# Layer normalisation of a convolution branch: the channel tiles summed before the product with the mean matrix

## The chip, the core and the metric

The kernel runs on one core of a Trainium2 chip. The metric is the device time of one execution in microseconds (us). The engines are PE (matrix products), DVE (VectorE), ACT (ScalarE), POOL (GpSimd) and SP, which only issues DMAs. Each has its own instruction queue that runs in order; they wait for each other through semaphores.

## What is computed

The reference is one step of a two-layer decoder for a prompt of 1024 tokens and 8 samples of 4 tokens, 1056 token columns in all. Layer 0 projects the input (1024 channels) onto 3352 columns that feed a convolution branch and a sparse attention branch. The part around the change is the convolution branch:

```python
y = lax.conv_general_dilated(u_ext, conv_w[:, None, :], (1,), 'VALID', ...) + conv_b   # 512 channels
return jax.nn.silu(layer_norm(y, ln_g, ln_b)) * jax.nn.silu(a_gate)

def layer_norm(x, g, b):
    mu = x.mean(-1, keepdims=True)
    var = jnp.square(x - mu).mean(-1, keepdims=True)
    return (x - mu) * lax.rsqrt(var + LN_EPS) * g + b
```

Mean and variance go over the 512 channels of a token. After it come attention, the output projection, the pooling layer 1 and its output projection.

## The kernel before

Activations lie with channels on the 128 partitions and tokens along the free axis. So the 512 channels of the convolution are four tiles `Y[:, i, :]` (i = 0 to 3) of 128 x 1056 float32, and the 1056 columns are worked on in three parts c = 0, 1, 2 of CH = 352.

The input projection runs over weight blocks m = 0 to 26 (function `one(m)` on PE, L754): 24 steps of three matmuls each (8 contraction tiles kk, three high and low products), into PSUM banks 0 to 2 for even m and 3 to 5 for odd m. The weight block m is rounded by ACT (`high`, L358, tile WH), its remainder taken by DVE or by POOL (`low`, L287, tile WL; POOL does m = 25 and 26 here), and after the products ACT moves the result out (`evac(m)`, L377).

The convolution's 30 later taps per tile are DVE instructions (L606) that run beside the projection and end shortly after block 23. The normalisation is then woven into blocks 24 and 25:

- `mean(c)` (L734): four float32 products of the matrix `meanm` (all entries 1/512) with `Y[:, 0..3, part c]`, added up in a PSUM bank. Each float32 product is issued as two matmuls, so a `mean` is 8 matmul instructions. The result is the mean over all 512 channels on every partition.
- DVE subtracts it from the four tiles (L641) and signals `s_yc`.
- `square(n)` on ACT (L417), n = 4c + i, writes the square of part c of tile i into one of the five buffers of SQ.
- `variance(c)` (L742): four products of `meanm` with the four squares, again 8 matmul instructions.
- `deviation(c)` on ACT (L424): the square root into RSTD. DVE takes the reciprocal (L646) and multiplies the four tiles (L648, `s_yn`).
- ACT applies scale, bias and SiLU to each whole tile (L484, `s_ys`), POOL multiplies by the gate (L346, `s_ya`).

The order on each queue is the order in the code. On PE: block 23, nine small transposes of the gates (L815), `mean(0)`, a wait for the gates' copy (`s_gtok`, L820, set by ACT at L470), block 24 with `mean(1)` before step kk = 2 and `mean(2)` before kk = 5, `variance(0)`, block 25 with `variance(1)` before kk = 3 and `variance(2)` before kk = 6, block 26, transposes of the value rows (L838), and then the attention. On ACT, block 24's evacuation and `high(26)` stand between the first five squares and the rest.

What follows blocks 24 to 26 is ordered by a planner for the attention, which the change does not touch; its first steps wait for the transposes of L838 and L832 (`s_tmt`) and for the convolution's last product (`s_ya`).

## Time and profile before

| | us |
|---|---|
| median of 3 runs | 1115.72 (1115.23 to 1117.55) |
| the profiled execution, its own time | 1120.08 |
| its span, first to last instruction | 1118.3 |
| PE busy | 1069.5 (96%) |
| DVE busy | 734.0 (66%) |
| ACT busy | 381.8 (34%) |
| POOL busy | 358.1 (32%) |

Busy time is a mean over stages with different limits. The stretch that matters here runs from 340 to 400 us of the span. All times at which something starts are counted from the span's start. The mean granted TensorE clock of the execution was 0.988 of full speed.

### The profile page before, as it was taken

What the parts mean: (1) busy time and instruction counts of PE and PEld (TensorE: products, weight loads), DVE (VectorE), ACT (ScalarE), POOL (GpSimd) and SP (SyncE); (2) the same over time, 40 slices, a digit from 0 to 9 for tenths busy, and PEclk for the clock granted to TensorE, in tenths of its full rate; (3) what the DMA queues carried; (4) which work ended last, traced back from release to release, by engine and by line L of the source; (5) the groups of instructions that cost most, each with busy time, mean ns of one, the idle gap of its engine ahead of it and who ended that gap; (6) DMA issues with size and microseconds to landing.
All of it is one profiled execution on the core that took longest, in us unless ns stands there. A gap on an engine that the chain in (4) does not pass through costs nothing.

```text
span 1118.3 us, 18968 instructions
## 1 busy us (share of the span) xinstructions
PE 1069.5 (96%) x7640; PEld 903.7 (81%) x7640; DVE 734.0 (66%) x1366; ACT 381.8 (34%) x805; POOL 358.1 (32%) x378
## 2 busy tenths in 40 slices
PE   6999999999999988999899989999999999999997
PEld 6888999999988954565556556787899999998875
DVE  3677889999885476676465766667546730258755
ACT  4201112123222554788466765411121121244000
POOL 3553630000000485665675454400023221309000
PEclk9999999999999988999899999999999999999998
DMA  8754511161421035300672027632221111142321
GB/s 235 239 162 144 167 60 38 40 227 51 122 43 20 1 101 174 115 2 1 229 258 81 2 94 236 162 130 85 76 76 39 55 38 32 32 151 76 128 84 61
DMA packets 85888, 113.73 MB, mean 102 GB/s; under 512 B 21952, under 2 KB 67144, under 8 KB 85727
## 3 DMA queue, kind: packets, MB, share of 16 engines
q1 hardware_dynamic: 71849, 69.51, 20.1%
q0 software_dynamic: 11776, 41.95, 11.1%
q10 hardware_dynamic: 2182, 1.16, 0.4%
q8 instruction: 55, 0.90, 0.3%
q14 instruction: 26, 0.21, 0.1%
HBM read 100.91 MB, written 16.64 MB: 105 GB/s over the span
## 4 chain that ended last, share of the span: by engine, by line
PE 85%; DVE 6%; issue 3%; DMA 3%; ACT 1%; POOL 1%; SPq 0%; DVEq 0%; POOLq 0%
PE PS L699 26%; PE PS L2059 15%; PE PS L1827 14%; PE PS L1314 5%; PE PS L1193 5%; PE PS L1175 4%; PE PS L687 3%; PE PS L1851 2%; PE PS L1231 2%; DMA TM<-in_state_win_kv 1%; DVE ACC L559 1%; PE PS L1840 1%; DMA XIN<-in_x_prompt 1%; PE PS L2039 1%; PE PS L1290 1%
## 5 line engine op out<-in xcount | busy, mean ns | idle before, releaser
L606 DVE SCALAR_TENSOR_TENSOR Y<-U,SM,Y 128x1024 f32<-128x1024 f32 x120 | 147.9, 1293 | 0.3
L699 PE MATMUL PS<-XH,WH 128*128 128x352 f32 (+1 forms) x648 | 146.9, 331 | 0.0
L699 PE MATMUL PS<-XL,WH 128*128 128x352 f32 (+1 forms) x648 | 144.0, 326 | 0.0
L699 PE MATMUL PS<-XH,WL 128*128 128x352 f32 (+1 forms) x648 | 143.2, 325 | 0.0
L699 PEld LDWEIGHTS PS<-XH,WH 128*128 128x128 f32 (+1 forms) x648 | 107.9, 186 | 2.7
L699 PEld LDWEIGHTS PS<-XH,WL 128*128 128x128 f32 (+1 forms) x648 | 108.1, 185 | 1.4
L699 PEld LDWEIGHTS PS<-XL,WH 128*128 128x128 f32 (+1 forms) x648 | 107.9, 185 | 1.4
L2166 POOL TENSOR_TENSOR WL<-WRAW,WH 128x1024 fp32r<-128x1024 f32 x14 | 37.4, 2675 | 210.8 <-ACT WH L2111 210.8
L559 DVE SCALAR_TENSOR_TENSOR ACC<-PS,SM,ACC 128x508 f32<-128x508 f32 x124 | 86.9, 741 | 25.1 <-PE PS L687 20.6
L290 POOL TENSOR_TENSOR WL<-WRAW,WH 128x1024 fp32r<-128x1024 f32 x12 | 28.7, 2391 | 231.8 <-ACT WH L363 231.1
L1314 PE MATMUL PS<-KV,Q 64*128 64x512 f32 (+3 forms) x384 | 79.4, 497 | 0.4 <-DVE STAT L1412 0.3
L2059 PE MATMUL PS<-XH,WH 128*128 128x352 f32 x360 | 77.2, 323 | 0.0
L2059 PE MATMUL PS<-XH,WL 128*128 128x352 f32 x360 | 77.1, 323 | 0.0
L2059 PE MATMUL PS<-XL,WH 128*128 128x352 f32 x360 | 77.1, 323 | 0.0
L1193 PE MATMUL PS<-PT,TM 128*64 128x256 f32 x528 | 72.5, 396 | 1.2 <-DVE BG L1508 1.1
L1827 PE MATMUL PS<-WOH,XH 128*128 128x512 f32 x224 | 71.0, 398 | 0.0
L1827 PE MATMUL PS<-WOL,XH 128*128 128x512 f32 x224 | 69.8, 393 | 0.0
L1827 PE MATMUL PS<-WOH,XL 128*128 128x512 f32 x224 | 69.5, 391 | 0.0
L1347 DVE COPY PT<-PS 128x512 f32<-128x512 f32 (+1 forms) x80 | 51.6, 645 | 21.6 <-PE PS L1175 9.1
L1569 POOL TENSOR_SCALAR PRS<-PRS,STAT,GTOK 128x512 f32<-128x512 f32 (+7 forms) x64 | 51.8, 820 | 41.5 <-DVE STAT L1408 41.1
L1314 PEld LDWEIGHTS PS<-KV,Q 64*128 64x128 f32 x384 | 39.4, 192 | 31.8 <-issue 18.0
L2059 PEld LDWEIGHTS PS<-XH,WL 128*128 128x128 f32 x360 | 61.0, 188 | 0.0
(333 smaller groups left out, 2040.3 us busy)
## 6 DMA issues: line engine op xcount, KB each, us to landing
WRAW<-in_w_in_even SPq DMA_DIRECT2D x16, 512.0 KB
WRAW<-in_w_in_odd SPq DMA_DIRECT2D x16, 512.0 KB, 4.1
TM<-in_state_win_kv SPq DMA_DIRECT2D x12, 512.0 KB
XIN<-in_x_prompt SPq DMA_DIRECT2D x8, 512.0 KB, 12.7
WRAW<-in_w_in_even SPq DMA_DIRECT2D x16, 256.0 KB
XR<-in_x_prompt SPq DMA_DIRECT2D x8, 512.0 KB, 3.5
layer_out<-R SPq DMA_DIRECT2D x8, 512.0 KB, 2.6
XR<-layer_out SPq DMA_DIRECT2D x8, 512.0 KB, 3.3
```

Source lines behind the costliest of these rows:

```text
L559: ins = v.scalar_tensor_tensor(acc, rows, weight, acc, ALU.mult, ALU.add)
L606: v.scalar_tensor_tensor(dst, src, CWT[:, i, t:t + 1], dst, ALU.mult, ALU.add).then_inc(s_cv, 1)
L687: ins = pe.transpose(PS[:, 6 + x, b * P:b * P + P], XC[:, load % 2, b, 256 * j + P * x:256 * j + P * x + P], ident[:, :])
L699: ins = pe.matmul(PS[0:mcols, 3 * slot + c, 0:CH], w[:, slot, kk, 0:mcols], x[:, kk, c * CH:(c + 1) * CH], start=(kk == 0 and n == 0), sto ...
L1175: ins = pe.transpose(PS[0:rows, 4 + a, c:c + 64], x[half, :], ident[half, half])
L1193: ins = pe.matmul(PS[hb:hb + HD, 6, 256 * gp:256 * gp + 256], v, PT[k % 2][0:rows, j, 256 * h:256 * h + 256], start=first, stop=(br == CMPB))
L1314: ins = pe.matmul(PS[:, row_bank[j] + b // 512, 0:w], Q[hb:hb + HD, g, tok(qt)], keys[:, k0 + b:k0 + b + w], start=True, stop=True)
L1347: ins = copy(out[:, :, :, a, :], PS[0:rows, 4 + a, 0:256 * k].rearrange("p (t x q) -> p t x q", t=k, q=64))
L1569: po.tensor_scalar(x, x, RCP[:, stat(p, h):stat(p, h) + 1], GTOK[:, qt, c:c + 1], ALU.mult, ALU.mult)\
L1827: ins = pe.matmul(PS[0:n, b0 + hf, :], x[:, kk, tok(tile)], w[:, kk, hf * 512:hf * 512 + 512], start=(kk == 0 and i == 0), stop=(kk == KT ...
L2059: ins = pe.matmul(PS[:, b0 + c, 0:CH], w[:, slot, kk, :], x[:, kk, c * CH:(c + 1) * CH], start=(kk == 0 and n == 0), stop=(kk == KT - 1 an ...
L2166: po.tensor_tensor(WL[:, m % 2, :, :], WRAW[:, m % 2, :, :], WH[:, m % 2, :, :].bitcast(F32), ALU.subtract).then_inc(s_wl2, 1)
```

## The change

The four tiles of Y are added up before the product with `meanm`, so that `mean(c)` is one product (two matmul instructions) instead of four. The sum goes into the tile SUM, which lies where SIG lay: POOL adds tiles 0 and 1, once the first two taps' tiles are done (`s_conv` 2), the sample columns are there (`s_cs`), and the stores of KWROW and SROW, which lie in the same place, have landed (`s_vrow`). DVE adds tiles 2 and 3 after its last tap. The squares are treated alike: DVE adds the four squares of a part with three instructions (`sum_squares`), and `variance(c)` is one product. All three means stand before step kk = 2 of block 24, `variance(0)` before kk = 6, and `variance(1)` and `variance(2)` before kk = 1 and 2 of block 25. `mean(2)` uses bank 5, so block 25 waits until DVE has read it (`s_yc` 3). ACT does all twelve squares and the first deviation before `high(26)`, and evacuates block 24 only after the three deviations. POOL's masks wait for the third mean. Three semaphores are reused from the input loads: s_half, s_sum and s_sqs are the semaphores s_xin6, s_xin7 and s_xin8 in the rows below; s_vrow is s_xin0.

```diff
--- before.py
+++ after.py
@@ -147,7 +147,7 @@
             "s_const", "s_rows", "s_pt", "s_stc", "s_idx", "s_small", "s_smalle", "s_xt", "s_xh", "s_xl")
         s_xin = sems(*[f"s_xin{i}" for i in range(NTT)])
         X_IN = 16
-        s_vrow, s_urow, s_rowst, s_winst, s_wc0, s_wc1 = s_xin[0:6]
+        s_vrow, s_urow, s_rowst, s_winst, s_wc0, s_wc1, s_half, s_sum, s_sqs = s_xin
         s_raw = sems("s_raw0", "s_raw1")
         s_xc = sems("s_xc0", "s_xc1")
         (s_cpt, s_cp, s_past, s_kcts, s_vcn) = sems("s_cpt", "s_cp", "s_past", "s_kcts", "s_vcn")
@@ -177,9 +177,15 @@
         VCN = at("VCN", [P, DB, P], F32, 105600)
         SMP = at("SMP", [P, 2, DS, DB], F32, GTOK_AT)
         NSQ = 5
+
+        def squared(n):
+
+            return 3 * (n // 4) + (1, 3, 2)[n % 4]
+
         SQ = at("SQ", [P, NSQ, CH], F32, 136256)
         RSTD = at("RSTD", [P, 3, CH], F32, 136256 + NSQ * CH * 4)
-        LN_BANK = ((6, 7, 6), (7, 6, 7))
+        LN_BANK = ((6, 7, 5), (6, 7, 6))
+        SUM = SIG
         TM = at("TM", [P, NTT, 768], F32, 164832)
 
         def values_copied(eng):
@@ -337,9 +343,14 @@
                 low(po, m)
                 if m < 8:
                     gather(m)
+            po.wait_ge(s_vrow, X_IN + 48)
+            po.wait_ge(s_conv, 2)
+            po.wait_ge(s_cs, 1)
+            po.tensor_tensor(SUM[:, :], Y[:, 0, :], Y[:, 1, :], ALU.add).then_inc(s_half, 1)
             for m in range(LOW_DVE[1], NM + 1):
                 po.wait_ge(s_wl, m)
                 low(po, m)
+            po.wait_ge(s_mean, 3)
             pool_masks(po, link)
             for i in range(4):
                 po.wait_ge(s_ys, i + 1)
@@ -417,12 +428,14 @@
             def square(n):
                 c, i = n // 4, n % 4
                 act.wait_ge(s_yc, c + 1)
-                if n >= NSQ:
-                    act.wait_ge(s_sqr, n - NSQ + 1)
+                if n == 8:
+                    act.wait_ge(s_sqr, 1)
+                elif n >= NSQ:
+                    act.wait_ge(s_sqs, X_IN + squared(n - NSQ))
                 act.activation(SQ[:, n % NSQ, :], Y[:, i, c * CH:c * CH + CH], ACT.Square).then_inc(s_sq, 1)
 
             def deviation(c):
-                act.wait_ge(s_sqr, 4 * c + 4)
+                act.wait_ge(s_sqr, c + 1)
                 act.activation(RSTD[:, c, :], PS[:, LN_BANK[1][c], 0:CH], ACT.Sqrt, bias=EPSC[:, :]).then_inc(s_stdc, 1)
 
             def rows_out(m):
@@ -444,7 +457,7 @@
 
             for m in range(NM + 1):
                 evac(m)
-                if m + 2 <= NM:
+                if m + 2 < NM:
                     high(m + 2)
                 if m in (3, 4, 6, 8):
                     i = (3, 4, 6, 8).index(m)
@@ -468,14 +481,11 @@
                     act.wait_ge(s_gt, 1)
                     act.activation(GTOK[:, 0:8, :], PS[:, 7, 0:192].rearrange("p (t g) -> p t g", g=24), ACT.Copy)
                     act.activation(GTOK[0:NSAMP, 8, :], PS[0:NSAMP, 7, 192:216], ACT.Copy).then_inc(s_gtok, 1)
-                    for n in range(NSQ):
+                    for n in range(12):
+                        if n == 9:
+                            deviation(0)
                         square(n)
-                elif m == 24:
-                    for n in range(NSQ, 9):
-                        square(n)
-                    deviation(0)
-                    for n in range(9, 12):
-                        square(n)
+                    high(NM)
                     deviation(1)
                     deviation(2)
                 elif m == 25:
@@ -634,12 +644,31 @@
                     taps(5)
             taps(len(TAPS))
 
-            for c in range(3):
+            v.wait_ge(s_half, X_IN + 1)
+            link(v.tensor_tensor(SUM[:, :], SUM[:, :], Y[:, 2, :], ALU.add))
+            v.tensor_tensor(SUM[:, :], SUM[:, :], Y[:, 3, :], ALU.add).then_inc(s_sum, 1)
+
+            def centre(c):
                 v.wait_ge(s_mean, c + 1)
                 cols = slice(c * CH, c * CH + CH)
                 for i in range(4):
                     ins = v.tensor_tensor(Y[:, i, cols], Y[:, i, cols], PS[:, LN_BANK[0][c], 0:CH], ALU.subtract)
                 ins.then_inc(s_yc, 1)
+
+            def sum_squares(c):
+                sq = [SQ[:, (4 * c + i) % NSQ, :] for i in range(4)]
+                v.wait_ge(s_sq, 4 * c + 4)
+                v.tensor_tensor(sq[1], sq[1], sq[0], ALU.add).then_inc(s_sqs, 1)
+                v.tensor_tensor(sq[3], sq[3], sq[2], ALU.add).then_inc(s_sqs, 1)
+                v.wait_ge(s_sqs, X_IN + 3 * c + 2)
+                v.tensor_tensor(sq[3], sq[3], sq[1], ALU.add).then_inc(s_sqs, 1)
+
+            centre(0)
+            centre(1)
+            sum_squares(0)
+            centre(2)
+            sum_squares(1)
+            sum_squares(2)
             for c in range(3):
                 cols = slice(c * CH, c * CH + CH)
                 v.wait_ge(s_stdc, c + 1)
@@ -732,24 +761,16 @@
             pe.wait_ge(s_const, 2)
 
             def mean(c):
+                pe.wait_ge(s_sum, X_IN + 1)
+                pe.matmul(PS[:, LN_BANK[0][c], 0:CH], meanm[:, :], SUM[:, c * CH:(c + 1) * CH], start=True, stop=True)\
+                    .then_inc(s_mean, 1)
+
+            def variance(c):
+                pe.wait_ge(s_sqs, X_IN + 3 * c + 3)
                 if c == 2:
-                    pe.wait_ge(s_yc, 1)
-                for i in range(4):
-                    ins = pe.matmul(PS[:, LN_BANK[0][c], 0:CH], meanm[:, :], Y[:, i, c * CH:(c + 1) * CH], start=(i == 0),
-                                    stop=(i == 3))
-                ins.then_inc(s_mean, 1)
-
-            def variance(c):
-                if c == 0:
-                    pe.wait_ge(s_yc, 2)
-                elif c == 1:
-                    pe.wait_ge(s_yc, 3)
-                else:
                     pe.wait_ge(s_stdc, 1)
-                for i in range(4):
-                    pe.wait_ge(s_sq, 4 * c + i + 1)
-                    pe.matmul(PS[:, LN_BANK[1][c], 0:CH], meanm[:, :], SQ[:, (4 * c + i) % NSQ, :], start=(i == 0),
-                              stop=(i == 3)).then_inc(s_sqr, 1)
+                pe.matmul(PS[:, LN_BANK[1][c], 0:CH], meanm[:, :], SQ[:, (4 * c + 3) % NSQ, :], start=True, stop=True)\
+                    .then_inc(s_sqr, 1)
 
             def one(m, between=()):
 
@@ -815,12 +836,11 @@
                 ins = pe.transpose(PS[0:n, 7, 24 * tt:24 * tt + 24], G[:, tok(tt)], ident[0:24, 0:24])
             ins.then_inc(s_gt, 1)
             pe.wait_ge(s_vc, 1)
-            pe.wait_ge(s_conv, 4)
-            mean(0)
             pe.wait_ge(s_gtok, 1)
-            one(24, ((2, mean, 1), (5, mean, 2)))
-            variance(0)
-            one(25, ((3, variance, 1), (6, variance, 2)))
+            pe.wait_ge(s_ev, 2 + 24)
+            one(24, ((2, mean, 0), (2, mean, 1), (2, mean, 2), (6, variance, 0)))
+            pe.wait_ge(s_yc, 3)
+            one(25, ((1, variance, 1), (2, variance, 2)))
             one(NM)
 
 
@@ -832,7 +852,7 @@
                         ins = pe.transpose(PS[0:NSAMP, 7, j * P:j * P + P], KV[:, x, SEQ:T], ident[:, :])
                 else:
                     if n == 3:
-                        pe.wait_ge(s_stdc, 2)
+                        pe.wait_ge(s_stdc, 3)
                     for t in range(2):
                         for a in range(2):
                             ins = pe.transpose(PS[:, 3 + n, (2 * t + a) * P:(2 * t + a) * P + P], KV[:, 3 + 2 * a, tok(2 * n + t)],
```

PE's queue from the gate transposes into block 24, before (XH, XL are the high and low activations, WH, WL the weights):

```order
L815 MATMUL PS<-ident,G 32x24
L738 MATMUL PS<-Y,meanm 128x352 [waits s_conv,s_vc]
L738 MATMUL PS<-Y,meanm 128x352 x3
L699 MATMUL PS<-XH,WH 128x352 [waits s_ev,s_wl,s_gtok]
L699 MATMUL PS<-XH,WH 128x352 x2
L699 MATMUL PS<-XL,WH 128x352 x3
L699 MATMUL PS<-XH,WL 128x352 x3
L699 MATMUL PS<-XH,WH 128x352 x3
L699 MATMUL PS<-XL,WH 128x352 x3
L699 MATMUL PS<-XH,WL 128x352 x3
L738 MATMUL PS<-Y,meanm 128x352 x4
```

And the same place now:

```order
L836 MATMUL PS<-ident,G 32x24
L728 MATMUL PS<-XH,WH 128x352 [waits s_wl,s_ev,s_gtok,s_vc]
L728 MATMUL PS<-XH,WH 128x352 x2
L728 MATMUL PS<-XL,WH 128x352 x3
L728 MATMUL PS<-XH,WL 128x352 x3
L728 MATMUL PS<-XH,WH 128x352 x3
L728 MATMUL PS<-XL,WH 128x352 x3
L728 MATMUL PS<-XH,WL 128x352 x3
L765 MATMUL PS<-SIG,meanm 128x352 [waits s_xin7] x3
```

Four products that stood between the transposes and the wait for `s_gtok` are gone, and the three single products of the means stand together behind the first 18 matmuls of block 24.

ACT's queue from the gates' copy to block 24's evacuation and the SiLU, before:

```order
L470 ACTIVATE GTOK<-PS 32x24
L422 ACTIVATE SQ<-Y 128x352 [waits s_yc] x5
L415 ACTIVATE BG<-PS 128x1056 [waits s_mm]
L363 ACTIVATE WH<-WRAW 128x1024 [waits s_mm,s_raw0]
L422 ACTIVATE SQ<-Y 128x352 [waits s_sqr,s_yc] x4
L426 ACT_TABLE_LOAD
L426 ACTIVATE RSTD<-PS,EPSC 128x352 [waits s_sqr]
L422 ACTIVATE SQ<-Y 128x352 [waits s_sqr,s_yc] x3
L426 ACTIVATE RSTD<-PS,EPSC 128x352 [waits s_sqr] x2
L415 ACT_TABLE_LOAD
L415 ACTIVATE BG<-PS 128x1056 [waits s_mm]
L484 ACTIVATE Y<-Y,SM 128x1056 [waits s_yn] x4
```

And now:

```order
L483 ACTIVATE GTOK<-PS 32x24
L435 ACTIVATE SQ<-Y 128x352 [waits s_yc] x5
L435 ACTIVATE SQ<-Y 128x352 [waits s_xin8,s_yc] x3
L435 ACTIVATE SQ<-Y 128x352 [waits s_sqr,s_yc]
L439 ACT_TABLE_LOAD
L439 ACTIVATE RSTD<-PS,EPSC 128x352 [waits s_sqr]
L435 ACTIVATE SQ<-Y 128x352 [waits s_xin8,s_yc] x3
L374 ACTIVATE WH<-WRAW 128x1024 [waits s_mm,s_raw0]
L439 ACTIVATE RSTD<-PS,EPSC 128x352 [waits s_sqr] x2
L426 ACT_TABLE_LOAD
L426 ACTIVATE BG<-PS 128x1056 [waits s_mm] x2
L494 ACTIVATE Y<-Y,SM 128x1056 [waits s_yn] x4
```

The evacuation of block 24 and the rounding of weight block 26 moved behind the squares; the number of table loads is the same.

## Rows read from the trace of the kernel before

**Rows 1.** The page, its chain that ended last: shares of the span by engine.

```profile
PE 85%; DVE 6%; issue 3%; DMA 3%; ACT 1%; POOL 1%; SPq 0%; DVEq 0%; POOLq 0%
```

**Rows 2.** The chain, 310 to 420 us: start, us, engine, tile, line, count.

```profile
347.65 2.56 PE PS L738 x8
...
353.13 2.37 PE PS L738 x8
...
382.27 14.41 PE PS L699 x90
396.68 1.76 PE PS L838 x16
```

**Rows 3.** Instructions of L738: shortest, median, longest in ns.

```profile
L738 PEld LDWEIGHTS PS<-Y,meanm x24: 186/190/191, 347.6 to 361.4; 128*128 128x128 f32 x24
L738 PE MATMUL PS<-Y,meanm x24: 457/459/563, 347.6 to 361.7; 128*128 128x352 f32 x24
```

**Rows 4.** ACT in order of time: start, us, work, [idle before it].

```profile
348.01 1.05 ACT L363 ACTIVATE WH<-WRAW 128x1024 fp32r<-128x1024 f32 x1
...
349.16 0.16 ACT L470 ACTIVATE GTOK<-PS 32x24 f32<-32x24 f32 x1
352.10 1.66 ACT L422 ACTIVATE SQ<-Y 128x352 f32<-128x352 f32 x4 [2.77 <-DVE Y L641]
...
370.11 1.28 ACT L426 ACT_TABLE_LOAD   x1
371.41 0.56 ACT L426 ACTIVATE RSTD<-PS,EPSC 128x352 f32<-128x352 f32 x1
...
385.19 1.05 ACT L415 ACTIVATE BG<-PS 128x1056 f32<-128x1056 f32 x1 [1.03 <-PE PS L699]
386.14 4.74 ACT L484 ACTIVATE Y<-Y,SM 128x1056 f32<-128x1056 f32 x4
```

**Rows 5.** DVE in order of time, 225 to 320 and 320 to 410 us.

```profile
301.10 1.23 DVE L290 TENSOR_TENSOR WL<-WRAW,WH 128x1024 fp32r<-128x1024 f32 x1 [1.64 <-ACT WH L363]
...
338.77 8.45 DVE L606 SCALAR_TENSOR_TENSOR Y<-U,SM,Y 128x1024 f32<-128x1024 f32 x7
350.25 1.81 DVE L641 TENSOR_TENSOR Y<-Y,PS 128x352 f32<-128x352 f32 x4 [3.03 <-PE PS L738]
...
372.00 2.35 DVE L646 RECIPROCAL RSTD<-RSTD 128x352 f32<-128x352 f32 x1 [7.96 <-ACT RSTD L426]
374.38 2.21 DVE L648 TENSOR_TENSOR Y<-Y,RSTD 128x352 f32<-128x352 f32 x4
```

**Rows 6.** POOL in order of time, 320 to 410 us.

```profile
349.20 2.38 POOL L290 TENSOR_TENSOR WL<-WRAW,WH 128x1024 fp32r<-128x1024 f32 x1 [188.24 <-ACT WH L363]
...
387.48 9.72 POOL L346 TENSOR_TENSOR Y<-Y,AG 128x1056 f32<-128x1056 f32 x4 [9.64 <-ACT Y L484]
398.91 2.07 POOL L1597 CAST XH<-Y 128x1056 fp32r<-128x1056 f32 x2 [1.71 <-PE PS L832]
```

**Rows 7.** A POOL and a DVE instruction near 114 us, and DVE's L1513.

```profile
112.72 2.40 POOL L290 TENSOR_TENSOR WL<-WRAW,WH 128x1024 fp32r<-128x1024 f32 x1 [9.56 <-ACT WH L363]
...
113.99 2.21 DVE L606 SCALAR_TENSOR_TENSOR Y<-U,SM,Y 128x1024 f32<-128x1024 f32 x1
...
L1513 DVE TENSOR_TENSOR XL<-Y,XH x4: 1242/1250/1749, 407.7 to 427.0; 128x1056 fp32r<-128x1056 f32 x4
```

**Rows 8.** The stores of L253: their issue, and time to landing.

```profile
L253 SPq DMA_DIRECT2D out<-SROW x2: 423/462/502, 291.0 to 291.5; - x2
...
DMA to landing us min/median/max: 1.8/2.0/2.2
```

**Rows 9.** Stretches: length, busy PE PEld DVE ACT POOL, granted clock, DMA share, GB/s.

```profile
408.00:412.00 4.00, 1.78 (x16) 0.91 (x12) 3.86 (x10) 2.06 (x11) 4.00 (x5) 1.00 0.00 0
412.00:416.00 4.00, 2.54 (x24) 1.96 (x22) 3.80 (x9) 0.98 (x2) 3.83 (x5) 0.62 0.11 20
...
942.00:944.00 2.00, 1.06 (x10) 0.97 (x11) 0.89 (x1) 0.79 (x1) 1.13 (x1) 1.00 0.00 0
```

## The prediction

> **What bounds the kernel now.** I first read the chain that ended last: PE holds 85% of the span [rows 1]. Then I read that chain from 310 to 420 us, because the share of an engine over the whole span says nothing about one stage. There PE never pauses: matmul group follows matmul group up to the transposes of L838, and the normalisation's products stand in the chain themselves, the first group with 2.56 us, one of the other five (they are equal) with 2.37 [rows 2]. So in this stretch a microsecond taken from PE is a microsecond of the kernel, if nothing else becomes later than PE. ACT and DVE are then read in order of time, since the change gives them work: both idle for whole microseconds between their pieces of the normalisation, each time waiting for PE or for each other [rows 4, 5]. POOL has been idle for 188 us before 349.20 [rows 6]. Last comes the granted clock, at full speed here (942 us stands for such a place) and at 0.62 in a stretch that follows one with PE little used [rows 9].
>
> **What is removed.** Six groups of 8 matmuls: 2.56 + 5 x 2.37 = 14.41 us of the chain [rows 2]. One matmul costs 2.37 / 8 = 0.296 us of PE's time, though its own duration reads 457 ns, since neighbours overlap [rows 3].
>
> **What is added on PE.** Six products, 12 matmuls: 12 x 0.296 = 3.55 us. They now stand in four groups (the three means together, each variance alone). Should each group show an uncovered weight load of 0.19 us [rows 3], that is 0.76 more; the five old groups had the same two borders and their price includes them, so I take 3.55, with 3.5 to 4.3 as bounds.
>
> **A wait that loses its cover.** Before, `mean(0)` filled PE from 347.65 to 350.2. Block 24 waits for `s_gtok`, which ACT gives at 349.16 + 0.16 = 349.32, behind block 23's evacuation and `high(25)` [rows 4]. Now nothing stands in between: PE stops at 347.65, and its first weight load can start at about 349.4, the first matmul 0.19 later. Cost: 349.6 - 347.65 = 1.95 us. Bounds: 1.7 (weights loaded ahead of the wait) to 2.2.
>
> The sum on PE: 14.41 - 3.55 - 1.95 = 8.9 us.
>
> **What could be later than PE.** I follow the new order through with the durations of the rows. PE's block steps cost 14.41 / 90 = 0.160 us per matmul, 1.44 per kk of nine [rows 2].
> - Sum: the taps end at 347.22 [rows 5]. A DVE addition of two float32 tiles of 1056 columns costs 1.24 us [rows 7], so the two end at 349.8. PE reaches the means at 349.6 + 2.9 = 352.5: slack 2.7.
> - POOL's addition: by its product of two such tiles 9.72 / 4 = 2.4 us [rows 6]. Its last condition is the landing of SROW, 291.5 + 2.2 = 293.7 [rows 8]; so it runs near 294 to 296, and DVE needs it at 347.2. It holds up POOL's `low(25)`, which is asked for only at 349.2 [rows 6]. Free.
> - Means end at 353.2; a subtraction of four tiles costs 1.81, four squares 1.66 [rows 4, 5]. Subtract part 0 to 355.1, part 1 to 356.8; squares 0 to 3 end at 356.8; the three additions of squares (about 0.45 each by 1.81 / 4, with the last waiting for the second: 1.5 us, between 1.35 and 1.8) end at 358.4. PE reaches `variance(0)` at 360.0: slack 1.6.
> - Part 2 is subtracted by 360.1; PE starts block 25 at 363.5: slack 3.4.
> - Square 8 waits for `variance(0)`, 360.8, and ends at 361.3; the table load of 1.28 and the root of 0.56 [rows 4] bring 363.2; squares 9 to 11 end at 364.4; the additions at 365.9. PE reaches `variance(2)` at 367.0: slack 1.1, the tightest.
> - Behind the squares stands `high(26)` (1.05 us, to 365.3), then POOL's `low(26)` (2.4, to 367.9), then block 24's evacuation with its table load (to 370.7). PE wants the last two at 376.2, the start of block 26. Hidden.
> - DVE's three reciprocals and products, 3 x (2.35 + 1.83), end at 378.4. Block 25's evacuation ends at 377.5 (385.19 + 1.05 before), so the SiLU starts about 8.8 us earlier, and POOL's four gate products (9.72) end at 388.4, before the transposes that POOL's first cast waits for: 398.75 - 8.9 = 389.8. Before, it also waited 1.71 us for them [rows 6].
> So PE stays ahead in the chain by no wait, and what follows 396.7 starts 8.9 us earlier. Everything there waits for these engines and not for a fixed time: the DMAs of the attention are issued after `s_tmt`.
>
> The profiled execution took 1120.08, 4.36 above the median of the runs shown (1115.72); the difference is applied to the median: 1115.72 - 8.9 = **1106.8 us** (in a profiled execution like this one, 1111.2).
>
> **A rule that speaks against the change.** The trace shows DVE's tap of two SBUF operands, issued at 113.99 while POOL's L290 ran until 115.12, taking 2.21 us instead of the 1.2 of its neighbours (8.45 / 7) [rows 5, 7]: it stood still until POOL was through. The Trainium skill says so in "SBUF — State Buffer" (the section on the shared port pair): a DVE instruction with two SBUF inputs and a GpSimd instruction that reads SBUF exclude each other, and whichever starts first holds the interface for its whole length. The trace agrees with it. If the two never excluded each other, the sum would be 8.9 us; by the row at 113.99 it is 8.9 or 7.3, as follows. All eleven new additions on DVE have two SBUF operands like that tap, so three meetings have to be looked at, by the rows:
> - POOL's addition at 294 against the taps: one tap loses up to 2.4 us. DVE idles 1.64 us before its next L290 at 301.10 [rows 5] and again before later ones, so the taps still end near 347.2; if nothing were made up, the sum would be ready at 352.2, still before 352.5.
> - DVE's second addition (348.5 to 349.8) against POOL's `low(25)` at 349.2: DVE starts first, POOL may have to wait half a microsecond; block 25 wants it at 363.
> - The last addition of the squares against `low(26)`. Square 11 ends at some time E. DVE's third addition starts at E + 1.0 (two additions and a wait), POOL at E + 1.1 (`high(26)`, then 0.14 as from 349.06 to 349.20). They are 0.1 us apart. That is the first rival.
>
> **Rival 1: POOL wins that meeting.** `low(26)` runs first, to 367.9; DVE's third addition ends at 368.4 and PE waits at `variance(2)` from 367.0 to 368.6. Price 1.6 us, time 1108.4. For it: 0.1 us is less than I can claim from rows. Against: both sides count from the same event. Chance 22%.
>
> **Rival 2: the new stop brings the clock down.** PE is idle for 1.95 us near 348 to 349.6, right after small transposes. In 408 to 412 PE was busy 1.78 of 4 us, and the granted clock then averaged 0.62 over the next 4 us [rows 9], so part of the stretch ran at the 1.2 GHz level. Against it: in 942 to 944 PE was busy 1.06 of 2 us, with a gap of 1.3, and the clock stayed at 1.00 [rows 9]. The new stop lies between the two. The row's fall cost 0.38 x 4 = 1.5 us in its 4 us; I take twice that length, 3 us, time 1110. Chance 12%.
>
> **Rival 3: given back later.** The attention's plan runs with other phases between clock falls and transfers than before, and loses or gains up to 3 us; or POOL's chain (SiLU, gate products) and not the transposes sets its start. Slack there is 1.4 us, so this needs two small delays. Time 1109 to 1113. Chance 10%; no net change at all (within the bound below) 4% more.
>
> **Rival 4, the other side: slower.** One mechanism: the clock falls at the stop of 348 us and does not come back while blocks 24 run. It decides from the point where more than 8.9 us of full-speed work runs at half speed. If all of block 24 with its products (11.55 + 2.37 = 13.9 us) ran at 1.2 GHz, it would cost 13.9 us: 1120.7. Against it: PE is busy without a pause after the stop, and the low clock in the rows came back before such a length in the view I have. Chance 3%.
>
> That the change does not do what it says can be set aside: the order shows single products in place of four.
>
> **How the numbers follow.** Forecast 49%, rival 1 22%, rival 2 12%, rival 3 10% and 4%, rival 4 3%. About 0.2% (2.2 us) is what a measurement of this kernel can tell from no change. Faster by more than that, under 1113.5: 0.91; within it 0.05; slower 0.04. The range: the forecast with PE's bounds (-0.3, +1.0) and 2 us either way for what the attention does with another phase gives 1104.3 to 1109; rivals 1 and 2 lie at 1108.4 and 1110. I take 1104 to 1111.
>
> **What the profile after would show.** Matmuls with `meanm`: 12 instead of 48. A gap on PE of about 1.9 us before block 24, released by ACT's gate copy. No wait of PE at the means; none, or 1.6 us, at `variance(2)`, and in the second case POOL's `low(26)` starting before DVE's last addition of squares. POOL's `low(25)` at nearly 3 us instead of 2.4, if DVE held the interface. The transposes near 387.8 instead of 396.7. Clock 1.00 from 350 to 380. I am wrong if PE waits for `s_sum` or at `variance(0)`, if the transposes come 8.9 us earlier and the end does not, or if the clock falls after 348.

## The result

The changed kernel takes 1101.37 us (median of 4 runs, 1100.62 to 1102.54), the kernel before 1115.53 beside it. The ratio is 0.9879 with a 95% interval of 0.9846 to 0.9912: 14 us less, against a forecast of 8.9. The profiled execution took 1101.45 us, with a span of 1099.7.

Lines of `kernel.py` from 700 on lie about 20 further down now: L738 and L742 are L765 and L772, L838 is L858, L1290 is L1310. The chain that ended last, 325 to 391 us, after (start, us, engine, tile, line, count), answers to [rows 2]:

```profile
325.28 23.10 PE PS L728 x144
348.43 0.93 issue
349.35 1.05 ACT WH L374
...
350.77 3.16 PE PS L728 x18
353.93 1.77 PE PS L765 x6
355.70 5.77 PE PS L728 x36
361.47 0.59 PE PS L772 x2
...
366.39 0.59 PE PS L772 x2
...
368.43 0.59 PE PS L772 x2
369.02 20.18 PE PS L728 x126
389.20 1.76 PE PS L858 x16
```

The products cost 1.77 + 3 x 0.59 = 3.54 us where they cost 14.41, and PE pauses once, ahead of block 24. The rows of PE, DVE and POOL in order of time, after (the idle time before a row and who ended it in brackets) answer to [rows 4 to 6]:

```profile
350.77 0.72 PE L728 MATMUL PS<-XH,WH 128*128 128x352 f32 x3 [1.77 <-ACT GTOK L483]
```

```profile
350.01 1.26 DVE L649 TENSOR_TENSOR SIG<-SIG,Y 128x1056 f32<-128x1056 f32 x1
354.56 3.54 DVE L655 TENSOR_TENSOR Y<-Y,PS 128x352 f32<-128x352 f32 x8 [3.29 <-PE PS L765]
...
366.71 0.52 DVE L664 TENSOR_TENSOR SQ<-SQ 128x352 f32<-128x352 f32 x1
367.15 2.35 DVE L675 RECIPROCAL RSTD<-RSTD 128x352 f32<-128x352 f32 x1
```

```profile
350.54 2.99 POOL L296 TENSOR_TENSOR WL<-WRAW,WH 128x1024 fp32r<-128x1024 f32 x1 [52.19 <-ACT WH L374]
366.77 2.72 POOL L296 TENSOR_TENSOR WL<-WRAW,WH 128x1024 fp32r<-128x1024 f32 x1 [13.24 <-ACT WH L374]
...
380.18 9.74 POOL L357 TENSOR_TENSOR Y<-Y,AG 128x1056 f32<-128x1056 f32 x4 [3.68 <-ACT Y L494]
391.43 1.06 POOL L1617 CAST XH<-Y 128x1056 fp32r<-128x1056 f32 x1 [1.51 <-PE PS L852]
```

Nothing but the gates' copy stops PE; POOL still waits for the transposes and not the other way round. The granted clock was 1.00 from 345 to 390 us in this execution.

The rest of the difference lies behind this stage. The attention runs from the value rows' transposes to the output projection. First and last start of their matmuls, before (three numbers ahead: shortest, median, longest in ns):

```profile
L838 PE MATMUL PS<-ident,KV x16: 270/272/274, 396.5 to 398.2; 128*128 128x128 f32 x16
L1827 PE MATMUL PS<-WOH,XH x224: 389/395/498, 695.1 to 1098.0; 128*128 128x512 f32 x112
```

and after:

```profile
L858 PE MATMUL PS<-ident,KV x16: 270/273/274, 389.0 to 390.7; 128*128 128x128 f32 x16
L1847 PE MATMUL PS<-WOH,XH x224: 389/395/504, 676.4 to 1079.4; 128*128 128x512 f32 x112
```

The stage gives 396.5 - 389.0 = 7.5 us, the attention shrinks from 298.6 to 287.4 us, and the distance at the end of the projection (18.6) is still the one at its start (18.7). So the two profiled executions differ by 18.6, of which 11.2 came from code that the change does not touch. (The one of before was 4.4 above its median.) The largest single part sits 144 us into the attention before and 140 after, where PE waits for a reload of the window rows (the rows of the sliding window, loaded into the tile TM from `in_state_win_kv`; there are two such reloads in the attention). Before:

```profile
540.49 1.07 PE L1290 MATMUL PS<-TM,PTW 128*32 128x128 f32 x8 [2.68 <-DMA TM<-in_state_win_kv]
```

```profile
536.00:538.00 2.00, 1.81 (x14) 1.11 (x12) 0.34 (x2) 1.36 (x4) 1.59 (x2) 1.00 0.98 287
538.00:540.00 2.00, 0.00 (x0) 0.00 (x0) 0.92 (x6) 0.65 (x4) 0.00 (x0) 0.81 0.90 309
540.00:542.00 2.00, 1.51 (x16) 1.50 (x16) 0.68 (x8) 1.26 (x7) 1.76 (x3) 0.50 1.00 410
542.00:544.00 2.00, 2.00 (x20) 0.91 (x18) 0.49 (x2) 0.00 (x0) 0.74 (x2) 0.50 0.57 180
544.00:546.00 2.00, 2.00 (x14) 1.09 (x12) 0.86 (x3) 0.60 (x1) 1.54 (x3) 0.50 0.72 246
546.00:548.00 2.00, 2.00 (x30) 1.48 (x28) 0.00 (x0) 0.00 (x0) 1.39 (x3) 0.99 0.86 298
```

and after (the stretches' columns are those of [rows 9]):

```profile
528.99 0.63 PE L1310 MATMUL PS<-TM,PTW 128*32 128x128 f32 x8 [1.19 <-DMA TM<-in_state_win_kv]
```

```profile
526.00:528.00 2.00, 1.80 (x16) 1.07 (x16) 1.41 (x7) 2.00 (x7) 1.66 (x2) 1.00 0.98 344
528.00:530.00 2.00, 1.01 (x18) 0.84 (x18) 0.86 (x8) 1.50 (x8) 1.81 (x3) 1.00 1.06 380
530.00:532.00 2.00, 2.00 (x26) 1.18 (x26) 1.28 (x4) 0.60 (x1) 1.45 (x5) 1.00 0.98 390
```

Before, PE stands still for 2.68 us and then works some 6 us at the 1.2 GHz level (granted clock 0.50). After, the wait is 1.19 us and the clock stays at 1.00. Counted at equal matmuls, the two are 5.0 us further apart behind this place than ahead of it, and 2.0 more at the second reload (waits of 1.26 and 1.04 us, 250 to 275 us into the attention). The other 4 us of the 11.2 arise elsewhere: 2.2 within its first 100 us, 1.8 near 165 us. Before's clock was also at 0.50 for 3.4 us from 40 us on and after's was not, and PE's waits for DVE at PT come to 5.8 us before and 3.0 after. The core's DMA queues together moved 242 GB/s in the ten microseconds around these transfers before (531 to 541) and 281 after (521.5 to 531.5).

### The profile page after: what moved, and what is told of

Same layout as the page of the kernel before. It is cut to its first block, busy times and chain, and to the rows that moved or that the text cites. A ratio compares the mean times of both kernels' runs of the same rounds, so it can differ in the third digit from the quotient of the medians.

```text
span 1099.7 us, 18908 instructions
## 1 busy us (share of the span) xinstructions
PE 1052.6 (96%) x7604; PEld 893.4 (81%) x7604; DVE 744.4 (68%) x1377; ACT 381.9 (35%) x805; POOL 364.8 (33%) x379
## 4 chain that ended last, share of the span: by engine, by line
PE 84%; DVE 6%; DMA 3%; issue 2%; ACT 2%; POOL 1%; SPq 0%; DVEq 0%; POOLq 0%
PE PS L728 26%; PE PS L2079 16%; PE PS L1847 14%; PE PS L1213 5%; PE PS L1334 5%; PE PS L1195 4%; PE PS L716 3%; PE PS L1871 2%; DMA WRAW<-in_w_in_even 2%; PE PS L1251 2%; PE PS L1860 1%; DVE ACC L569 1%; DMA TM<-in_state_win_kv 1%; PE PS L2059 1%; PE PS L1310 1%
## 5 line engine op out<-in xcount | busy, mean ns | idle before, releaser
L616 DVE SCALAR_TENSOR_TENSOR Y<-U,SM,Y 128x1024 f32<-128x1024 f32 x120 | 150.1, 1312 | 0.3
L2186 POOL TENSOR_TENSOR WL<-WRAW,WH 128x1024 fp32r<-128x1024 f32 x14 | 37.5, 2675 | 208.7 <-ACT WH L2131 208.7
L1334 PE MATMUL PS<-KV,Q 64*128 64x512 f32 (+3 forms) x384 | 75.7, 482 | 0.4 <-DVE STAT L1432 0.4
L2079 PEld LDWEIGHTS PS<-XL,WH 128*128 128x128 f32 x360 | 60.9, 188 | 0.0
```

Of the source, the lines that this page charges most:

```text
L616: v.scalar_tensor_tensor(dst, src, CWT[:, i, t:t + 1], dst, ALU.mult, ALU.add).then_inc(s_cv, 1)
L1334: ins = pe.matmul(PS[:, row_bank[j] + b // 512, 0:w], Q[hb:hb + HD, g, tok(qt)], keys[:, k0 + b:k0 + b + w], start=True, stop=True)
L2079: ins = pe.matmul(PS[:, b0 + c, 0:CH], w[:, slot, kk, :], x[:, kk, c * CH:(c + 1) * CH], start=(kk == 0 and n == 0), stop=(kk == KT - 1 an ...
L2186: po.tensor_tensor(WL[:, m % 2, :, :], WRAW[:, m % 2, :, :], WH[:, m % 2, :, :].bitcast(F32), ALU.subtract).then_inc(s_wl2, 1)
```

## The experiments

Runs of one session share a chip and the runs of the kernel before. Two sessions were longer as a whole (the kernel before at 1120.45 and 1122.24 us, against 1115.6 to 1116.0 in the other three), so kernels are compared within a session or by their ratio to before. "Attention" is the length defined above, in the profiled execution.

### Session 1 (before: 1115.63): is it the products, the additions, or another place of the code?

**e1_before_again**: the kernel before, unchanged. 

> The kernel before, unchanged, for a second profile of it. The attention, from the value-row transposes to the first product of the output projection, took 298.6 us in the profile of before and 287.4 in that of after. Theory A (the attention is shorter after the change by a cause that repeats): this profile shows 296 to 300 us again, and time 1115.5. Theory B (the attention's length scatters from execution to execution by its clock falls and transfers): this profile shows another length, anywhere in 287 to 300, at a median of 1115.5.

Measured: 1115.47 us (1113.44 to 1119.24), ratio 0.9994 (0.9969 to 1.0019). Attention 292.7, outside theory A's 296 to 300; PE waits 4.7 us in two waits for the window reload, the longer one at the second:

```profile
664.32 1.07 PE L1290 MATMUL PS<-TM,PTW 128*32 128x128 f32 x8 [2.89 <-DMA TM<-in_state_win_kv]
```

The clock fell to 0.50 for 3.4 us at each. This execution (1115.98 us) lies near the median, and is the fairer one to compare: its attention is 5.3 us longer than the changed kernel's, 0.7 us shorter up to the first reload, 2.1 longer at it and 3.9 at the second. The 2.2 and 1.8 us elsewhere in the first profile of before are absent here, and PE's waits for DVE at PT are 3.1 us.

**e2_after_padded**: the changed kernel, each product issued four times.

```diff
-                pe.matmul(PS[:, LN_BANK[0][c], 0:CH], meanm[:, :], SUM[:, c * CH:(c + 1) * CH], start=True, stop=True)\
-                    .then_inc(s_mean, 1)
+                for _ in range(4):
+                    ins = pe.matmul(PS[:, LN_BANK[0][c], 0:CH], meanm[:, :], SUM[:, c * CH:(c + 1) * CH], start=True, stop=True)
+                ins.then_inc(s_mean, 1)
...
```

(`variance` in the same way.)

> The kernel after with each of its six products with the mean matrix issued four times into the same bank, so that PE does the 36 matmuls more that the change removed (10.7 us), while sums, orders and waits stay as in after. Theory A1 (the attention gains because it starts earlier): it starts as late as before, so the gain goes: 1101.4 + 10.7 + 5.4 = 1117.5. Theory A2 (the gain comes with the change's other edits and not with the time of the start) and theory B: 1101.4 + 10.7 = 1112.1.

Measured: 1117.3 us (1109.92 to 1121.53), ratio 1.0006 (0.9977 to 1.0035). The 36 extra matmuls are 36 x 0.296 = 10.7 us of PE; the kernel gives back 15.9. The 1117.3 is no less than before's 1115.63, so the new additions on DVE and POOL bring nothing by themselves, and PE's issue alone takes the gain away, with more than its own length. The profiled execution happened to be the shortest of the ten (1109.92): its attention is 285.7, with 0.6 us of window waits, so this profile does not show the long attention that the median of 1117.3 points to.

**e3_before_one_product**: the kernel before with one product (tile 3) where it has four, no sums; the normalisation is incomplete.

```diff
-                for i in range(4):
-                    ins = pe.matmul(PS[:, LN_BANK[0][c], 0:CH], meanm[:, :], Y[:, i, c * CH:(c + 1) * CH], start=(i == 0),
-                                    stop=(i == 3))
-                ins.then_inc(s_mean, 1)
+                pe.matmul(PS[:, LN_BANK[0][c], 0:CH], meanm[:, :], Y[:, 3, c * CH:(c + 1) * CH], start=True, stop=True)\
+                    .then_inc(s_mean, 1)
...
```

(`variance` in the same way, behind a wait for all four squares.)

> The kernel before with one product in place of four in each mean and variance (of tile 3 alone, so the normalisation is left incomplete), without the sums on POOL and DVE. PE does 36 matmuls less (10.7 us) and waits for the gates' copy for 1.2 us behind the shorter first mean. Theory A1: 1115.5 - 9.4 - 5.4 = 1100.7. Theory A2 and B: 1115.5 - 9.4 = 1106.1.

Measured: 1101.0 us (1098.6 to 1102.25), ratio 0.9874 (0.9825 to 0.9924), attention 286.3. Removing products alone gives the whole gain, in the old order of ACT and DVE. (The ratio's interval is as wide as 11 us.)

**e4_late_wait**: the changed kernel with the wait for the gates' copy moved from block 24's start to its first mean.

```diff
             def mean(c):
+                pe.wait_ge(s_gtok, 1)
+                pe.wait_ge(s_ev, 2 + 24)
                 pe.wait_ge(s_sum, X_IN + 1)
...
-            pe.wait_ge(s_gtok, 1)
-            pe.wait_ge(s_ev, 2 + 24)
             one(24, ((2, mean, 0), (2, mean, 1), (2, mean, 2), (6, variance, 0)))
```

> The kernel after with PE's wait for the gates' copy moved from ahead of block 24 to ahead of the three means, whose bank it protects. The stop of PE before block 24 was 1.77 us idle and 2.4 from the last transposes to the first matmul. If PE's path alone counts: 1101.4 - 2.0 = 1099.4, transposes 2.0 us earlier. If the chain of sums and squares were the real limit behind it (slack 1.1 us at the last variance): PE waits at the means or at the last variance and 0 to 1 us remain of the gain.

Measured: 1099.4 us (1097.69 to 1101.05), ratio 0.9861 (0.9812 to 0.991). The stop is gone; its chain reads

```profile
348.30 0.63 PE PS L838 x9
348.93 3.11 PE PS L728 x18
352.04 1.77 PE PS L767 x6
```

The transposes of the value rows start at 387.1, 1.9 us earlier than in the changed kernel.

### Session 2 (before: 1116.04): the start, the count of instructions, or the reload?

**e5_late_start**: POOL first fills XH and XL, so that everything starts later.

```diff
+            po.memset(XHf[:, :, :], 0.0)
+            po.memset(XLf[:, :, :], 0.0)
             link(po.memset(ident[:, :], 0.0))
```

> The kernel after, but POOL first fills the tiles XH and XL with zeros (about 17 us) before it makes the identity matrix that PE's first transposes need. Everything then runs later by the part of this that the first input transfers do not hide, 5 to 12 us; instructions of PE, their number and their order stay as in after. Theory A1 (the attention's length depends on when, counted from the execution's start, it begins): if it begins at 396 to 400 us as before the change, it takes 290 to 299 us in the profile and the executions scatter by 8 us or more, as those of before did (1108.1 to 1121.6 over 19). Theory A3 (it depends on the number of instructions ahead of it): it stays at 286 to 288 us and the executions within 4 us of each other.

Measured: 1105.57 us (1103.78 to 1108.82), ratio 0.9914 (0.9889 to 0.9939). The attention starts at 392.2, only 3.2 later than after, and takes 288.1. Such a later start alone does not bring the long attention back; the shift was smaller than meant, so the test is a weak one.

**e6_more_instructions**: the changed kernel with the nine gate transposes issued five times, 72 more PE instructions (each transpose is a weight load and a matmul), as many as the change removed.

```diff
-            for tt in range(NTT):
+            for _ in range(5):
+                for tt in range(NTT):
...
```

> The kernel after with the nine small transposes of the gates issued five times, so that PE has 36 matmuls and 36 weight loads more ahead of the attention, as many as before the change, in 2.5 us instead of 10.7. The attention begins near 391.5. Theory A1: its length stays at 286 to 288, time 1101.4 + 2.5 = 1103.9, executions within 4 us. Theory A3: it behaves as before the change, time 1101.4 + 2.5 + 5 = 1109, executions scattered over 8 us.

Measured: 1111.57 us (1108.21 to 1114.81), ratio 0.9962 (0.994 to 0.9984). The transposes of the value rows start at 390.8, 1.8 later than after, 1.5 of it from a clock fall at block 24. The attention takes 296.2: 1.8 us ahead of it come with 9 more behind, and the clock falls at both reloads (for 6.8 and 3.4 us). Its waits of PE:

```profile
PE PS L1311 <- DMA TM<-in_state_win_kv: 6.7, 2, 3.5
```

(us in total, times, longest), where the changed kernel has

```profile
PE PS L1310 <- DMA TM<-in_state_win_kv: 2.2, 2, 1.2
```

**e7_before_no_reload** and **e8_after_no_reload**: both kernels without the later window loads; SP only gives the semaphores, and the products read the rows of other samples.

```diff
                 sp.wait_ge(s_pvq, 5 * a + 1)
-                sp_windows(sp, 2 * a)
+                for i in range(2):
+                    sp.sem_inc(s_wc[i], 16)
```

> The kernel before without the reload of the sliding-window rows of samples 0, 1, 4 and 5 before the last value products (their semaphores are raised by SP alone, the products read the rows of other samples). In the profile of before PE waited 2.68 us for this transfer at 144 us into the attention and ran at the 1.2 GHz level for some 6 us behind it. Theory D (the attention's extra time and its scatter come from this wait and the clock fall that it triggers): 1108 to 1110, executions within 4 us, no fall of the clock at 138 to 150 us into the attention. If the transfers are only a symptom: 1115.5 less the waits themselves, 3.9 us, so 1111.6, and the scatter stays.

> The kernel after without the same reload. Its profile showed 2.2 us of waits for it and no clock fall. Theory D: 1101.4 - 2.2 = 1099.2, so that the distance to the kernel before without the reload becomes the 8.8 us of PE work alone. If the start decides over something else in the attention, the distance stays at 14.

Measured: 1107.41 us (1107.08 to 1109.02), ratio 0.9932 (0.9906 to 0.9957), attention 284.4; and 1100.42 us (1098.49 to 1100.79), ratio 0.9863 (0.9824 to 0.9902), attention 285.5. Without the reload the two kernels are 7.0 us apart instead of 14, and their attentions are alike. e8 shows something else at the stop before block 24:

```profile
350.56 0.85 PE L728 MATMUL PS<-XH,WH 128*128 128x352 f32 x3 [1.78 <-ACT GTOK L483]
```

```profile
350.00:352.00 2.00, 1.44 (x6) 1.48 (x7) 1.05 (x1) 0.46 (x3) 1.67 (x1) 0.74 0.02 0
352.00:354.00 2.00, 2.00 (x8) 2.00 (x8) 0.00 (x0) 0.00 (x0) 1.28 (x1) 0.50 0.03 1
354.00:356.00 2.00, 2.00 (x11) 1.68 (x10) 0.14 (x1) 0.00 (x0) 0.00 (x0) 0.90 0.05 1
```

Here the same stop did bring the clock down, and the first 18 matmuls of block 24 took 4.67 us instead of 3.16.

### Session 3 (before: 1120.45): PE's work or its number of instructions?

All with extra transposes ahead of block 24, 64 in e11, 128 in e9 (changed kernel), 92 in e10 (kernel before):

```diff
             pe.wait_ge(s_vc, 1)
+            for _ in range(128):
+                pe.transpose(PS[:, 6, 0:24], G[:, 0:P], ident[0:24, 0:24])
```

> The kernel after with 128 small transposes more (128 matmuls and 128 weight loads, 256 instructions, into a free bank) ahead of block 24. They take 9.0 us and hide the 1.8 us stop there: +7.2. Theory I (what counts is where PE's instruction packets, one per 256 instructions, fall against the window transfers): same remainder as after, so the attention stays at 286 to 288 us, time 1108.6, executions within 5 us. Theory N (any more instructions or a later start make it longer, as in the padded kernels): 1114 or more, executions scattered over 8 us.

> The kernel before with 92 small transposes more (184 instructions) ahead of its first mean. Before has 72 instructions more than after, so 72 + 184 = 256 brings it to after's remainder. The transposes take 6.4 us, of which nothing is hidden. Theory I: the attention shrinks from 292 to 298 us to 286 to 288, so the added work of 6.4 costs about 1: 1115.5 + 6.4 - 5.4 = 1116.5, executions within 5 us. Theory N: 1115.5 + 6.4 = 1121.9, scattered over 8 us.

> The kernel after with 64 small transposes more (128 instructions, 4.5 us, of which 1.8 hide the stop): +2.7. The instruction packet then comes some 6 us ahead of the window transfers. Theory I, if only a packet right ahead of the transfer is harmful: 1101.4 + 2.7 = 1104.1 and tight. If every packet ahead of it is harmful, or theory N: 1109 to 1110 and scattered.

**e12_after_again** is the changed kernel. 

> The kernel after, unchanged, in the same session: 1101.4, executions within 4 us of each other (1100.6 to 1102.5 in its four), attention 286 to 288 us. If its quick attention was luck, some executions reach 1105 to 1110.

Measured: e12 1109.4 us (1106.64 to 1111.23), ratio 0.9876 (0.9835 to 0.9918); e11 1113.28 (1111.01 to 1114.71), 0.9922 (0.9895 to 0.9949); e9 1119.65 (1117.96 to 1121.01), 0.9988 (0.9969 to 1.0008); e10 1129.14 (1127.07 to 1129.96), 1.0067 (1.0046 to 1.0088). The ratio of the changed kernel came back (11 us by medians), but its attention was 294.8, 7 to 8 longer than in the other sessions, and 294.7 to 295.8 in all four kernels, with window waits of at most 0.5 us. So these runs could not tell the theories apart: the waits that they were to lengthen or shorten were absent here. e9 costs 10.2 over e12, and its attention starts 9.8 later (401.3 against 391.5), so all of it lies in the stage: e9's extra transposes brought the clock down themselves. Stretches of 4 us of e9, columns as in [rows 9]:

```profile
345.30:349.30 4.00, 4.00 (x33) 3.78 (x33) 3.85 (x4) 0.60 (x1) 0.00 (x0) 1.00 0.00 0
349.30:353.30 4.00, 4.00 (x58) 4.00 (x57) 2.23 (x2) 1.66 (x4) 2.47 (x1) 0.81 0.02 0
353.30:357.30 4.00, 4.00 (x40) 4.00 (x40) 0.00 (x0) 0.00 (x0) 0.47 (x1) 0.50 0.07 5
357.30:361.30 4.00, 4.00 (x36) 3.95 (x36) 0.00 (x0) 0.00 (x0) 0.00 (x0) 0.50 0.00 0
361.30:365.30 4.00, 4.00 (x15) 4.00 (x15) 0.00 (x0) 0.00 (x0) 0.00 (x0) 0.50 0.00 0
365.30:369.30 4.00, 4.00 (x21) 3.37 (x20) 2.52 (x6) 0.67 (x2) 0.00 (x0) 0.98 0.00 0
```

By its records PE is busy throughout, and still has 13.7 us at half clock (by these rows 1.5 + 12 + 0.2). An experiment that adds such small transposes adds their clock fall too, which I had not reckoned with; e10 is spoiled by it as well (10.2 us at half clock; 10.2 us more in the stage for 6.4 us of added work). The unchanged kernel before has no profile in session 3.

### Session 4 (before: 1115.79): the main comparison again, in five rounds

**e13_after_five** is the changed kernel, **e14_padded_five** repeats e2, **e15_after_no_reload_five** e8, **e16_before_no_reload_five** e7.

> The kernel after, in one session with the next three, five rounds. If only PE's path counts (the 8.9 us of the stage): before less 8.9. If the attention reliably adds its part: before less 11 to 14.

> The kernel after with every product issued four times, as in e2. PE's path alone: after + 10.7, so before + 1.8 by its stop. With the attention's part given back: after + 16, so before + 2 to + 5; e2 had 1117.3 against 1115.6.

> The kernel after without the reload of window rows, as in e8. Its profiles showed 1 to 2 us of waits for the reload, so 1 to 2 us below e13 in the same session.

> The kernel before without the reload, as in e7. If the part of the difference beyond 8.9 us sits in that wait and the clock fall behind it, this kernel is 8 to 9 us above e15 and 7 to 8 us below before; if the attention's part is elsewhere, it is 11 to 14 us above e15.

| | median us (lowest to highest) | ratio to before | attention |
|---|---|---|---|
| before | 1115.79 (1108.19 to 1121.42) | | |
| e13, after | 1101.08 (1099.48 to 1102.32) | 0.9869 (0.9834 to 0.9904) | 286.7 |
| e14, padded | 1119.9 (1111.77 to 1123.62) | 1.0029 (0.9999 to 1.0059) | 291.4 |
| e16, before without reload | 1107.27 (1106.0 to 1109.86) | 0.9926 (0.9899 to 0.9953) | 286.8 |
| e15, after without reload | 1099.04 (1098.44 to 1100.96) | 0.9853 (0.9818 to 0.9887) | 285.1 |

With the reload the kernels are 14.7 us apart, without it 8.2. The reload costs the kernel before 8.5 us and the changed one 2.0. The scatter goes with it: 13 us over 20 runs of before, 4 over 9 without the reload. The padded kernel pays 18.8 us over e13 for 10.7 us of matmuls, and in its profiled execution the stop brought the clock down as in e8.

### Session 5 (before: 1122.24)

**e17_before_184_spread**: the kernel before with the 92 transposes of e10 in four groups of 23 between blocks.

```diff
+            def small():
+                for _ in range(23):
+                    pe.transpose(PS[:, 6, 0:24], ident[0:24, :], ident[0:24, 0:24])
...
```

> The kernel before with the same 184 PE instructions more as in e10, in four groups of 23 small transposes ahead of the transposes after block 20, after block 21, and ahead of blocks 23 and 24. Work 92 x 0.07 = 6.4 us. Theory I (the place of the instruction packets against the window transfers decides; 72 + 184 = 256 gives after's place): before + 6.4 - 6.5, so the same time as before within 2 us, executions within 5 us of each other. If added instructions only add their time: before + 6.4, and a scatter over 8 us as before has.

Measured: 1124.81 us (1121.04 to 1127.35), ratio 1.0016 (0.9999 to 1.0034), attention 295.5, window wait 0.5. It costs 1.8 us by the ratio for 6.4 us of added transposes, so something was given back: the whole interval lies below the 1.0057 that added work alone would give. But the attention is again the long one in both profiled kernels of session 5 (295.5 here, 294.4 in e18), and the expected small scatter was not reached (6.3 us). This is a hint and no proof.

**e18_late_wait_five** repeats e4. 

> The kernel after with PE's wait for the gates' copy ahead of the means instead of ahead of block 24, as in e4, which measured 1099.4 against 1101.4 for after. Expected before less 16.5, 1.5 to 2 us better than after's distance of 14.7.

Measured: 1107.2 us (1105.94 to 1107.52), ratio 0.9858 (0.9831 to 0.9886), 15.0 less than before where 16.5 was expected. The transposes of the value rows start at 387.8, with no stop and no clock fall ahead of them.

## Why the prediction was right, and where it failed

**The removed and added products: right.** 14.41 us became 3.54 (I said 3.55); no extra cost for borders of groups.

**The wait that lost its cover: right.** PE idles 1.77 us by its row. In e4 block 24 follows the nine transposes after 0.63 us; by that it could have started at 348.93 and started at 350.77, 1.84 us later, against 1.95 with 1.7 to 2.2 as bounds.

**The sum of 8.9 us on PE: right.** The attention starts 7.5 us earlier in the first pair, in an execution whose gate transposes came 1.35 us later than before's (348.30 against 346.95). From the first gate transpose to the first transpose of the value rows the stage takes 49.56 us in all four profiles of before and its version without reload, and 40.7 in the changed kernel where the clock stays up: 8.8 less. Over the profiled executions of the 1116-us sessions it starts at 396.5, 398.1, 398.2 and 398.0 in before and its version without reload (mean 397.7), and at 389.0, 387.8, 390.3 and 388.8 in the changed one (mean 389.0): 8.7. Without reload, the whole kernels differ by 7.0 and 8.2.

**What could be later than PE: right.** No wait at the means, the variances or block 25. `low(26)` ends at 369.5, long before block 26; POOL's gate products end at 389.9, and POOL's cast still waits 1.51 us for the transposes.

**The shared interface: right in kind.** POOL's `low(25)` took 2.99 us and `low(26)` 2.72 where 2.38 is its time alone [rows 6]: both met a DVE addition with two SBUF operands that had begun 0.53 and 0.06 us before them. POOL's addition of tiles 0 and 1, at 294.78, took 3.57 us instead of 2.43 beside the taps. This is as "SBUF — State Buffer" of the Trainium skill has it (the section on the shared port pair): the one that starts first holds the interface, the other stands still. Rival 1, in which POOL wins the meeting at 366.7, did not come: DVE began 0.06 us ahead.

**Rival 2, the clock falls at the stop: it does happen, but not always, and at half my price.** The fall is there in e8, e12 and e14, and absent after the same stop in the first profile, e2, e5, e13 and e15: 3 of 8. It costs 1.3 to 1.5 us on the first 18 matmuls where it occurs (4.47 to 4.67 us instead of 3.16), and the stage is 1.5 longer in e8 and e12 (42.3 us). I had 3, from a row that itself said 1.5. Rival 4, a fall that lasts through block 24, was not seen.

**The step that failed: what the attention does.** I granted it 2 us either way in the range, and in rival 3 up to 3 us ("loses or gains up to 3 us"), and applied the 8.9 us to the median as if all behind 396.7 moved along unchanged ("what follows 396.7 starts 8.9 us earlier", with the reason that everything there waits for these engines). It gained 5.3 us by the medians (14.2 - 8.9), as much as e1's attention is longer than the changed kernel's, and 11.2 in the profiled pair, where 4 us come from an execution of before that was itself 4.4 above its median. That term is mis-sized, and by it the time fell under the range. What is shown of its cause:
- It needs the products gone from PE's queue, not the new additions: e3 has the gain without them, e2 and e14 lose it with them.
- It needs the reload of the window rows: without it the kernels are 7 to 8 us apart, as the sum on PE says, and before scatters over 4 us instead of 13. The sizes come from two sessions that agree; the interval of each ratio is 6 to 9 us wide.
- It takes the form of two waits of PE for that transfer (2.68 and 1.26 us in before, 1.77 and 2.89 in e1, 3.54 and 3.15 in e6; 1.19 and 1.04, 0.93 and 0.64 in the changed kernel). At six of the seven waits of 1.7 us and more in these and e14 the clock fell to 0.50 for 3.4 to 6.8 us; at the thirteen of 1.3 us and less it did not.

Less firm is why the transfer comes late in the one and not in the other. A later start by 3.2 us did not do it (e5), 72 more PE instructions did (e6). I suspected the transfers that fetch instructions (16 KB each, the queue named "instruction" in the profile), whose place among the window's transfers moves with the number of PE instructions ahead of them. e9, e10 and e11 were to decide it and fell into a session in which no profiled kernel showed more than 0.5 us of it. The kept traces of the other sessions speak for it. Each reload is two transfers, and the times below are counted from the issue of the second:

| | first product on the rows | fetch of instructions starts | PE waits |
|---|---|---|---|
| before, e1, e6, e14 (8 reloads) | 7.1 to 8.9 us | -0.24 to 0.09 us | 1.3 to 3.5 us |
| after, e2, e3, e4, e5, e13 (12 reloads) | 5.6 to 6.6 us | 0.29 to 3.09 us | 0.3 to 1.2 us |

e2 and e14 are one kernel and stand on different sides. The fetch's place also moves as supposed: with 256 PE instructions more than the changed kernel has (e9, e10, e17) it starts 2.9 to 3.1 us behind the issue at the first reload and 0.6 to 0.7 at the second, where e12 has 3.1 and 0.7. So a fetch that starts with the reload goes with a late reload in all twenty cases. That it delays the reload is likely by this and not proven, since no run moved the fetch alone. In e11 it starts 1.3 and 1.9 us ahead of the issue and PE waits for neither reload. Nor do I know why the attention was 7 to 9 us longer for every profiled kernel in sessions 3 and 5. Against e13, e12 loses 3.3 us within the first 100 us of the attention and 1.8 near 165 us, the places at which the first profile of before lost its 4 us, and PE's waits for DVE at PT come to 5.8 to 6.3 us in both sessions as there.

The row that would have warned me stood in the trace of before: a wait of 2.68 us on a DMA with 6.8 us of lowered clock around it, in a profiled execution 4.4 us above its median. I read the stage of the change closely and the attention not at all.

**The better version.** e4 and e18, the changed kernel with the later wait, have ratios to before of 0.9861 and 0.9858, against 0.9879, 0.9876 and 0.9869 for the changed kernel. The intervals overlap, so the times alone don't separate them. The traces do for the stage: it takes 38.92 us in both, against 40.7 in the changed kernel (42.3 where its clock fell), so 1.8 us or more are gained there, and there is no stop at which the clock could fall.

## What to carry to other kernels

When PE is the bound, summing operands on idle engines ahead of a linear product buys PE's time almost one for one (10.9 us of products, 10.6 us of the stage in e4, 8.8 where the uncovered wait stayed), if every sum is ready in time; count that from rows, as here, and look for the wait that the removed work had covered, since it can often be moved behind work that doesn't need it. Then walk through what follows as well: where before waits for a transfer and the clock falls behind that wait, a shift by a few microseconds, or a few dozen instructions more or less, can be worth more than half of the change itself (5.3 us beside 8.8 here), and the range has to hold that price in both directions. A kernel that scatters over 13 us, as this one did until the reload was taken out, is a reason to look for such a place.

## What the runs showed of the hardware

- A long run of small transposes (24 columns) keeps PE busy at 4.00 of 4.00 us by its records, and the granted clock still fell to 0.50: for 13.7 us in e9 (128 of them in a row), for 10.2 in e10 (92).
- After the same stop of 1.77 us behind nine such transposes the clock was at 0.50 for 3.4 us in 3 of 8 profiled executions.
- A DMA reload with which a fetch of instructions started within 0.24 us was usable 7.1 to 8.9 us after its issue (8 cases), the same reload with the fetch 0.29 us or more behind it after 5.6 to 6.6 (12 cases).
- The kernel before, on the same chip, took 1115.63 us (19 runs) in one session and 1120.45 (21 runs) in another.
